# Layer 1 heads of a two-layer sequence model: the weights of both directions merged into one set for the value products, their low part on VectorE instead of GpSimd

## The reference, cut to what matters

```python
bcum = jnp.cumsum(fc, axis=-1)
log_d = jnp.where(mask, bcum[..., :, None] - bcum[..., None, :] + ic[..., None, :], -jnp.inf)
m_t = jnp.maximum(jnp.max(log_d, axis=-1), log_inter)
dmat = jnp.exp(log_d - m_t[..., None])
s = jnp.einsum('bhtd,bhsd->bhts', qc, kc) * dmat
num = jnp.einsum('bhts,bhsv->bhtv', s, vc) + ...
den = jnp.sum(s, -1) + ...
h = num / jnp.maximum(jnp.abs(den), jnp.exp(-m_t))[..., None]
...
yl_f, _ = scan_fn(*lat_f, st_f); yl_b, _ = scan_fn(*rev(lat_b), st_b)
y = from_heads(head_norm(h_f + h_b, LN_EPS, True)) * norm_g + skip * xc
return (y * jax.nn.silu(z)).astype(z.dtype)
```

## Time and profile before

| | us |
|---|---|
| median of three runs | 2862.51 (2860.26 to 2863.01) |
| profiled execution | 2845.39 |
| its span | 2843.5 |
| TensorE busy | 2487.3 (87%) |
| VectorE busy | 1573.6 (55%) |
| ScalarE busy | 901.1 (32%) |
| GpSimd busy | 729.5 (26%) |

### The profile page before, as it was taken

How to read it: one execution, slowest core, us unless ns; L and a number is a source line. 1 busy time by engine, 2 the same in 40 slices (tenths; PEclk the granted TensorE clock), 3 DMA queues, 4 the chain that set the end, 5 groups by cost and what they waited for, 6 DMA issues and landing times. The chain is left out here.

```text
span 2843.5 us, 53344 instructions
## 1 busy us (share of the span) xinstructions
PE 2487.3 (87%) x22670; PEld 2117.7 (74%) x22670; DVE 1573.6 (55%) x2510; ACT 901.1 (32%) x1504; POOL 729.5 (26%) x689
## 2 busy tenths in 40 slices
PE   6899999995898986777959999999599999995986
PEld 2577776775877774666848888878499999995865
DVE  3026878644456545764665665566455656565233
ACT  2113344231232333555123333332443443431310
POOL 1111110115757642000222222221222222221421
PEclk8999999997999997889979999999799999997998
DMA  7712545545333324114543444443724443312521
GB/s 276 247 53 76 152 133 156 172 141 170 94 104 95 109 67 121 30 61 170 128 85 129 161 161 161 154 167 122 278 88 149 145 142 134 104 60 94 191 93 60
DMA packets 338235, 372.05 MB, mean 131 GB/s; under 512 B 111247, under 2 KB 274838, under 8 KB 335438
## 3 DMA queue, kind: packets, MB, share of 16 engines
q1 hardware_dynamic: 336992, 365.31, 40.1%
q10 hardware_dynamic: 1006, 3.33, 0.3%
HBM read 228.76 MB, written 139.82 MB: 130 GB/s over the span
## 5 line engine op out<-in xcount | busy, mean ns | idle before, releaser
L3338 PE MATMUL PS<-V_hi,weights_hi 128*128 128x258 f32 x832 | 238.2, 286 | 10.4 <-DVE H L3549 6.9
L469 PE MATMUL PS<-hT_hi,w_in_hi 128*128 128x512 f32 (+1 forms) x640 | 239.6, 374 | 4.4 <-DVE q_out L3137 4.4
L3339 PE MATMUL PS<-V_lo,weights_hi 128*128 128x258 f32 x832 | 237.0, 285 | 0.0
L470 PE MATMUL PS<-hT_lo,w_in_hi 128*128 128x512 f32 (+1 forms) x640 | 236.3, 369 | 0.0
L471 PE MATMUL PS<-hT_hi,w_in_lo 128*128 128x512 f32 (+1 forms) x640 | 236.2, 369 | 0.0
L3340 PE MATMUL PS<-V_hi,weights_lo 128*128 128x258 f32 x832 | 236.1, 284 | 0.0
L469 PE MATMUL PS<-h_hi,w_in_hi 128*128 128x512 f32 (+1 forms) x624 | 229.9, 368 | 5.8 <-PEq L115 3.7
L3446 POOL TENSOR_TENSOR weights_lo<-weights,weights_hi 128x1664 fp32r<-128x1664 f32 x32 | 122.0, 3813 | 413.1 <-ACT weights_hi L3398 413.1
L470 PE MATMUL PS<-h_lo,w_in_hi 128*128 128x512 f32 (+1 forms) x624 | 225.7, 362 | 0.0
L471 PE MATMUL PS<-h_hi,w_in_lo 128*128 128x512 f32 (+1 forms) x624 | 225.3, 361 | 0.0
L3310 PE MATMUL PS<-Q_hi,K_hi 128*128 128x256 f32 x640 | 184.7, 289 | 28.5 <-DVE weights L3515 13.4
(11 more groups left out here) (453 smaller groups left out, 6178.4 us busy)
## 6 DMA issues: line engine op xcount, KB each, us to landing
chunk_in<-in_d SPq DMA_DIRECT2D x40, 512.0 KB, 3.4
w_in<-in_e_w_in_dram SPq DMA_DIRECT2D x30, 512.0 KB, 5.0
xnew<-in_o_w_in_dram SPq DMA_DIRECT2D x30, 512.0 KB, 6.4
in_d<-xnat SPq DMA_DIRECT2D x20, 640.0 KB, 6.0
modw<-in_mod_w_dram SPq DMA_DIRECT2D x12, 1024.0 KB, 9.7
xnat<-in_mod_w_dram SPq DMA_DIRECT2D x8, 1536.0 KB, 7.2
v_d<-xnew SPq DMA_DIRECT2D x16, 640.0 KB, 2.9
kh_d<-k_hi SPq DMA_DIRECT2D x16, 640.0 KB, 2.9
```

The costliest lines, as they stand in the source:

```text
L469: pe.matmul(PS[:, bank + off // 512, 0:n], wh[:, k], hh[:, k, t], start=(k == 0), stop=False)
L470: pe.matmul(PS[:, bank + off // 512, 0:n], wh[:, k], hl[:, k, t], start=False, stop=False)
L3338: pe.matmul(out, wh, VH[:, j, q], start=(j == seen[0]), stop=False)
L3339: pe.matmul(out, wh, VL[:, j, q], start=False, stop=False)
```

## The change

The two directions' weights are merged into one set of ten blocks before the value product. For each step the direction with fewer blocks (`minor`) is scaled by the ratio of the other direction's den to its own, and its three common blocks are added to the other's. Then one product over ten blocks, 512 columns wide, gives h times the major direction's den; the head norm removes this factor, with eps scaled by its square.

Since the sums are needed ahead of the product, they are computed on their own: `sum_weights` reduces each direction's slots over the slot index on VectorE, `den_sums` lets TensorE sum over the 128 keys (a product with ones, which hands the sum to all partitions, and a one-column one for the major direction's den), and `merge` on VectorE makes ratio, scaling and addition. The floors exp(-m) are needed as rows: they are written to memory once (`F_d`) and 32 small loads (`least_rows`) on ScalarE's queue bring them in. The low part moves from GpSimd to VectorE (`low`), H is evicted by ScalarE (`evict`), and `weights` gets a third buffer. Slots are renumbered so that the merged blocks are contiguous; for this one weighting a step is cut in two.

```diff
+    def minor(c):
+        return 0 if c < NCH // 2 + 1 else 1
...
+                def den_sums(n):
+                    c = n % TQ + CTXCH
+                    pe.wait_ge(s["summed"], n + 1)
+                    if n >= 2:
+                        pe.wait_ge(s["merged"], n - 1)
+                    pe.matmul(PS[:, 2 + n % 2, 0:2 * P], G.c("ones"), sums[:, n % 2].rearrange("p d t -> p (d t)"), start=True, stop=True)
+                    pe.matmul(PS[:, 2 + n % 2, 2 * P:2 * P + 1], sums[:, n % 2, 1 - minor(c)], G.c("ones")[:, 0:1],
+                              start=True, stop=True).then_inc(s["den_ps"], 1)
...
+                    if n >= 2:
+                        pe.wait_ge(s["h_ok"], n - 1)
+                    for j in range(NCH):
+                        wh, wl = (x[n % 2][:, merged_slot(c, j)] for x in (WH, WL))
+                        out = PS[:, n % 2, :]
+                        pe.matmul(out, wh, VH[:, j], start=(j == 0), stop=False)
+                        pe.matmul(out, wh, VL[:, j], start=False, stop=False)
+                        last = pe.matmul(out, wl, VH[:, j], start=False, stop=(j == NCH - 1))
...
                 for m in range(PAIRS):
                     h, i = m // PAIRS1, m % PAIRS1
+                    den_sums(2 * m)
+                    den_sums(2 * m + 1)
                     if m + 1 < PAIRS:
                         scores(m + 1, range(EARLY), turns)
                     values(2 * m)
...
+                    act.activation(WH[n % 2][:], W[:, n % 3, at:at + NCH], ACT.Copy).then_inc(s["w_hi"], 1)
+                    if n + 2 < STEPS:
+                        least_rows(n + 2)
...
+                    act.activation(H[:, i], PS[:, n % 2, :], ACT.Copy).then_inc(s["h_ok"], 1)
...
                 for n in range(STEPS):
                     h, i = n // TQ, n % TQ
-                    high(n)
+                    if n + 2 < STEPS:
+                        decay(n + 2)
                     if i == 0 and h:
                         values(h)
-                    if n + 2 < STEPS:
-                        decay(n + 2)
-                    if i == 5:
+                    high(n)
+                    if n:
+                        evict(n - 1)
+                    if i == 4:
                         root(h, 0)
-                    if i == 1 and h:
+                    if i == 0 and h:
                         root(h - 1, 1)
...
-                    pool.tensor_tensor(WL[n % 2][:], W[:, n % 2], WH[n % 2][:].bitcast(F32), ALU.subtract).then_inc(s["w_lo"], 1)
...
+                    for d in range(2):
+                        last = dve.tensor_reduce(sums[:, n % 2, d], W[:, n % 3, span(d, c)].rearrange("p s t -> p t s"), AX, ALU.add)
+                    last.then_inc(s["summed"], 1)
...
+                    step.add(dve.scalar_tensor_tensor(den[:, i:i + 1], col, -1.0, floor[:, 1 - b, c, h:h + 1], ALU.mult, ALU.max))
+                    step.link(dve.scalar_tensor_tensor(flow, row, -1.0, flow, ALU.mult, ALU.max))
+                    step.add(dve.tensor_tensor(den[:, i:i + 1], col, den[:, i:i + 1], ALU.max))
+                    step.link(dve.tensor_tensor(flow, row, flow, ALU.max))
+                    step.link(dve.reciprocal(low[:, b], low[:, b]))
+                    step.link(dve.tensor_tensor(low[:, b], low[:, b], low[:, 1 - b], ALU.mult))
+                    part = w[:, span(b, c)]
+                    step.link(dve.tensor_tensor(part, part, low[:, b][:, None, :].broadcast_to([P, part.shape[1], P]), ALU.mult))
+                    mine, other = w[:, NCH * (1 - b):NCH * (1 - b) + 3], w[:, NCH * b:NCH * b + 3]
+                    dve.tensor_tensor(mine, mine, other, ALU.add).then_inc(s["merged"], 1)
...
+                for m in range(PAIRS):
+                    h, i = m // PAIRS1, m % PAIRS1
+                    n0, n1 = 2 * m, 2 * m + 1
+                    sum_weights(n0)
+                    sum_weights(n1)
+                    if i == 2:
                         skip(2 * h)
                     if i == 0 and h:
                         skip(2 * h - 1)
+                    merge(n0)
+                    if i == 0 and h:
+                        low_values(dve, h)
+                    merge(n1)
+                    low(n0)
+                    if m:
+                        collect(n0 - 1)
+                    low(n1)
+                    if m + 1 < PAIRS:
+                        weigh_groups(m + 1, range(EARLY))
+                    if i == 2:
+                        normalize(h, 0)
+                    if i == 0 and h:
+                        normalize(h - 1, 1)
+                    collect(n0)
+                    if m + 1 < PAIRS:
+                        weigh_groups(m + 1, range(EARLY, NG))
+                    if i == 2:
                         take(h, 0)
+                        finish(h, 0)
+                    if i == 0 and h:
                         take(h - 1, 1)
                         finish(h - 1, 1)
+                    for n in (n0 + 4, n1 + 4):
+                        if n < STEPS:
+                            diag(n)
```

More of the change, by code:

```diff
@@ L3146 @@
 PQ = 2 * P
-VCOL = [0, P, 2 * P + 2, 3 * P + 2]
 SEEN = NCH + CTXCH + 1
@@ L3416, in _ @@
                     act.activation(gx[64:68, t], ga[64:68, u], ACT.Copy).then_inc(s["ga_ok"], 1)
+                act.wait_ge(s["rows_ok"], 3)
+                for d in range(2):
+                    q = slice(64 * d + 32, 64 * d + 36)
+                    act.activation(gl[q, CTX:], gx[q, CTX:], ACT.Exp).then_inc(s["f_ok"], 1)
                 values(0)
@@ L3512, in weigh @@
                         js = [j for j in uses(d, c) if 2 * g <= j < 2 * g + 2]
-                        if js:
-                            w = W[:, n % 2, slot(d, c, js[0]):slot(d, c, js[0]) + len(js)]
-                            last = dve.tensor_tensor(w, src[:, js[0] - 2 * g:js[-1] + 1 - 2 * g, a], w, ALU.mult)
+                        at = [slot(d, c, j) for j in js]
+                        if len(js) == 2 and at[1] != at[0] + 1:
+                            runs = [(js[:1], at[0]), (js[1:], at[1])]
+                        else:
+                            runs = [(js, at[0])] if js else []
+                        for keys, first in runs:
+                            w = W[:, n % 3, first:first + len(keys)]
+                            last = dve.tensor_tensor(w, src[:, keys[0] - 2 * g:keys[-1] + 1 - 2 * g, a], w, ALU.mult)
                     return last
@@ L3540, in collect @@
-                    step.wait()
-                    for d in range(2):
-                        step.add(dve.reciprocal(den[:, d, 1:2], den[:, d, 0:1]))
-                    step.wait()
-                    for half in range(2):
-                        step.add(dve.tensor_scalar(H[:, i, 2 * P * half:2 * P * half + 2 * P], PS[:, half, 0:2 * P], den[:, 0, 1:2], None, ALU.mult))
-                    step.wait()
-                    for half in range(2):
-                        hh = H[:, i, 2 * P * half:2 * P * half + 2 * P]
-                        ins = dve.scalar_tensor_tensor(hh, PS[:, 2 + half, 0:2 * P], den[:, 1, 1:2], hh, ALU.mult, ALU.add)
-                        if half:
-                            step.publish(ins, s["av_sb"], n + 1)
-                        else:
-                            step.add(ins)
```

153 lines of the change are left out of this document (82 added, 71 removed).

## The result

The changed kernel takes 2933.7 us (median of four runs) against 2861.4 us for the kernel before: 1.026 times, interval 1.023 to 1.029, or 72 us more. The forecast had the sign, and the range holds the time, but its sum was +31.6 us. More than half of the loss was not in it.

The account below looks back on a forecast made before the run. TensorE was taken to bound the step loop; -57.6 us of savings against waits of +66.5, +21.3, +7.6 and smaller terms gave +31.6 us, 2877.0 us profiled, 2894 us for the median, range 2848 to 2950.

Parts of the forecast that it names:

- Value products: TensorE, step loop: 30 matmuls of 512 columns replace 78; less the sums' matmuls, 1.8 us a step, 57.6 us gained.
- Reductions: VectorE, each step: two reductions over 13 slots, taken at one element a cycle, 1.9 us a step, at most 3.7.
- Reciprocal: VectorE, each merge: the 128-element reciprocal takes 0.29 us if it runs like its neighbours, otherwise 0.7 us.
- The ordinary pairs: Pairs without a turn: VectorE's 6.2 us fit within TensorE's 6.8 us odd-step product, 0.6 us to spare, no cost.
- The turns: Seven pairs that turn half a head: TensorE idles 6.9 us for the first sums, 0.4 more for the second.
- The clock: After a turn's idle stretch TensorE runs at half clock for 5 us, costing 2.2 us more a turn.
- First pair of heads 1 to 3: V_lo subtractions between merges: TensorE idles 3.7 us, 2.5 for the clock, last score group waits 0.9; +21.3 us in all.
- Third pair: Third pair of each head: ScalarE's root delays the weightings and last score group by 1.9 us, +7.6 us in all.
- Start: First pair's sums put 5.2 us plus 1.5 us of half clock ahead of the next pair's first scores, +6.7 us.
- dearer sums: Rival: VectorE's sums at the scan's rate cost 1.8 us more a step, 53 us over the loop, 2947 us; chance 0.18.
- Short pauses: Rival: TensorE's wait behind a turn and its half clock cost 3 us, not 9.5; 2849 us, faster; chance 0.13.
- cancelling: Rival: with pauses of about 5 us a turn, gain and loss cancel, time within 0.2%; chance 0.07.

Follow-up runs that it names:

- the forecast's prices: Changed kernel, reductions summing only 72 of 128 query columns from the third step on, reciprocal covering 20 of 128; 1.0108 times the kernel before, +31 us.
- the run with the stride alone: Changed kernel whose reductions read the same elements in address order, 4 instead of 512 bytes apart, forming other sums; 1.0157 times the kernel before, +45 us.
- the three combinations: Changed kernel with next pair's sums before the take and contiguous additions, plus finish moved (1.0007), low part on GpSimd (0.9981), or both (0.9899 times the kernel before).
- the fastest one: Changed kernel with sums before the take, contiguous additions, finish behind the next pair's low parts, low part on GpSimd; 0.9899 times the kernel before, -29 us.

## Why the prediction was right in sign and short in size

By its own steps:

- *Value products, -57.6 us.* Right. Where TensorE is again the bound, its busy time in the loop is 56.3 us lower.
- *Reductions, 1.9 us a step.* **This step failed.** 3.13 us, because a step of 512 bytes between elements costs 1.74 ns an element instead of 1.04. The stride alone is 30 us of the kernel's time. The bounds (1.9 to 3.7 us) held the measured price, the choice between them did not: it took one element a cycle from rows that all read neighbours, for work that does not.
- *Reciprocal, 0.29 us.* **Failed too**: 0.95 us, outside even the 0.7 us read from one to four elements, and against the forecast's claim that contiguous f32 operands of every kind run at one element a cycle. It is 13 us of the kernel's time.
- *The rest of the merge and the low part.* Right: 292 ns, 1488 ns.
- *The ordinary pairs, 0.6 us of room.* With 2.5 us more of reductions a pair they wait 0.61 to 1.05 us each, 6.9 us in all, so the room was nearer 1.6 us. With contiguous additions they wait for nothing.
- *The turns, 6.9 and 0.4 us.* Right in place and cause, 7.8 and 1.4 in size. By the forecast's own chain the first wait holds one step's sums, the second another's.
- *The clock, 2.2 us a turn.* The records show about 2 us: 1.2 to 1.6 on the score matmuls and 0.6 in the second step's sums (1.30 us from their start to the first score matmul, 0.67 at full clock). Adding all of it to the waits was too much: with full clock only 6 to 11 of the 15.4 us return, since TensorE then waits 1 us a turn longer for VectorE.
- *First pair of heads 1 to 3, 3.7 us, 2.5 for the clock, and 0.9.* 6.1 us, with 1.9 to 2.1 us for the clock behind it; the 0.9 us did not come. Without the reciprocal the wait was 4.1 us, with both of the forecast's prices 3.5.
- *Third pair, 1.9 us.* 1.95 us in three heads and 1.34 in one, but this is partly luck: with the forecast's prices it was 0.6 us in three heads and nothing in the fourth. The forecast has neither the 1.0 us in front of the even product nor the clock that falls behind these waits, 1.4 to 1.6 us in three heads.
- *Start, +6.7 us.* 13.0 us. TensorE is idle for 9.1 us more. 6.3 of them are the waits for the first sums (4.9 and 1.4 us, forecast 5.2). The other 2.8 are in waits that were there before: the first exponential begins 27.7 us after the first score matmul instead of 24.7, and ScalarE has two new operations for the rows of floors ahead of it, 2.1 us together. That these are the cause was not tested. The last 3.9 us are work: 2.7 for the sums' matmuls, which the forecast counts with the products, and the lower clock. The run with the forecast's prices does not bear on this, as it sums all columns in the first two steps.
- *Last pair and tail.* The wait for the high part is 7.0 us instead of 5.7, and the tail -2.1 instead of -1.7 us.
- *Carrying to the median by 17.1 us.* Against a profiled execution that quick, it moved no part of the difference, and the difference of medians (72 us) is that of the heads (74 us).
- *Arithmetic.* The sum adds up as written. The break-even is 5.0 us a turn rather than 5.1 (9.5 less 31.6 / 7), and the first pair's idle time works out as 3.8 us, not 3.7 (13.2 less 9.4).

Of the signs that it named, the waits before the sums stand in front of the turns and in front of the even product at the heads' starts, with the lower clock behind them. VectorE's share of the loop is 71%, not 80 or more. Two of its four signs of being wrong came: reductions of 3 us or more a step, and idle time in front of the sums of ordinary pairs. The chain of waits held; the price of VectorE's work on it did not.

Of the rivals, *dearer sums* was the case that came, at a price between its ends, with the reciprocal beside it. The rule cited there (the Trainium skill, Advanced Engine Details and Errata, Memory Cachelines: accesses that each go to another 16-byte line pay) decided right against the row that was preferred. No row of before shows such an access; the run with the stride alone shows the penalty as 0.70 ns an element, though not for groups of three (below). *Short pauses* and *cancelling* did not come, but the three combinations show what they would have taken: VectorE's queue cut in front of the sums and of the merge. No merge waited for its floors.

## What to carry to other kernels

A gain on the bounding engine is worth only what the engine that takes over its work has left between two meeting points, not on the average: VectorE was busy for 58% of the loop before and 71% after, and yet TensorE waited 8 us for it at seven places. Price what is added by its access pattern as well as by its element count, and when no row shows that pattern, take the dearer end for the forecast if the work stands in front of a wait. When a merge like this one loses, move what nobody waits for (finish, take) behind what the bounding engine waits for (sums, low part) before giving it up: here that turned +75 us into -29, together with cheaper sums and the low part back on GpSimd.

## What the runs showed of the hardware that was not expected

- A VectorE reduction of f32 elements 512 bytes apart takes 1.74 ns an element, over neighbours 1.04. With three elements per sum it is nearly free: 587 against 542 ns; with four, 1040 against 673.
- The reciprocal takes 154 ns for one element of a partition, 278 for 20 and 954 for 128: from 20 on, 6.3 ns an element, where the strided sums take 1.74 and the sums over neighbours 1.04.
- A VectorE multiplication of 128 elements in SBUF that starts while a GpSimd subtraction runs ends 0.15 us behind it, after up to 2.55 us; without one it takes 0.29 us (13 and 19 of 32 steps in the run with the low part on GpSimd, 16 and 16 in the fastest one). Weightings that read PSUM kept their 0.28 and 0.41 us beside a subtraction, and the reciprocal its 0.95.
- Pauses of TensorE well under the 4.14 us of the earlier trace rows were followed by matmuls at the lower clock: 2.15 and 1.3 to 2.0 us in a turn, and 1.0 and 1.95 us, 10 us of work apart, in the third pairs. Behind pauses of 0.45 and 0.5 to 0.7 us in a turn, and behind 0.6 us alone in the third pairs of the run with the forecast's prices, the matmuls came at full clock.
